# Attention's output, the MLPs and the residual in token-major form: activations as the stationary operand under 512-column weight moves, and per-token norms

## What is computed

```
mod_lat = (silu_c @ ada_w[i] + ada_b[i])[:, None, :]
sh1, sc1, g1, sh2, sc2, g2 = jnp.split(mod_lat, N_MOD, axis=-1)
h_lat = modulate(rms_norm(x, norm_mix_g[i]), sh1, sc1)
if mixer == 0:
    q_l, k_l, v_l = project_qkv(h_lat, ...); k_c, v_c = project_kv(h_ctx, ...)
    o_lat = latent_attention(q_l, k_l, v_l, k_c, v_c) @ attn_w_o[j]
else:
    o_lat = fourier_mix(h_lat, fourier_w_o[j])
x = x + g1 * o_lat
x = x + g2 * sq_relu_mlp(modulate(rms_norm(x, norm_mlp_g[i]), sh2, sc2), mlp_w1[i], mlp_w2[i])
...
return rms_norm(x, final_norm_g)
```

## Time and profile before

| | us |
|---|---|
| median of 3 runs | 2355.04 |
| lowest and highest run | 2353.82, 2355.83 |
| span of the profiled execution | 2354.1 |
| TensorE busy (matmul) | 2174.3 |
| VectorE busy | 1540.7 |
| ScalarE busy | 1057.1 |

### The profile page before, as it was taken

One profiled execution on the slowest core, in us unless ns is written; L12 is line 12 of the kernel. 1 busy time (PEld: TensorE's weight loads), 2 busy tenths in 40 slices (PEclk: granted clock), 3 DMA queues, 4 the chain that ended last, 5 costly groups with the idle time before them and its releaser, 6 DMA issues.

```text
span 2354.1 us, 40722 instructions
## 1 busy us (share of the span) xinstructions
PE 2174.3 (92%) x16563; PEld 2076.8 (88%) x16563; DVE 1540.7 (65%) x1499; ACT 1057.1 (45%) x1302; POOL 170.5 (7%) x245
## 2 busy tenths in 40 slices
PE   5989976679899999999999998989999998999998
PEld 3778864359899999989999988989999998999997
DVE  6868887878776666657777765865444445776554
ACT  4843333433454444444444445345444444444443
POOL 0000000000111111101111100000000000110000
PEclk9989987899999999999999999999999999999998
DMA  9957664248677777767777760965555556774551
GB/s 383 360 208 273 241 224 161 96 145 333 264 268 256 277 248 256 273 231 276 272 258 276 270 246 4 331 249 186 178 179 183 187 182 215 272 275 173 188 180 54
DMA packets 118782, 537.40 MB, mean 228 GB/s; under 512 B 8306, under 2 KB 9124, under 8 KB 97444
## 3 DMA queue, kind: packets, MB, share of 16 engines
q1 hardware_dynamic: 89472, 360.73, 43.0%
q0 software_dynamic: 27136, 167.78, 19.8%
q10 hardware_dynamic: 2084, 7.63, 0.8%
HBM read 534.01 MB, written 2.10 MB: 228 GB/s over the span
## 4 chain that ended last, share of the span: by engine, by line
PE 85%; DVE 9%; ACT 3%; issue 2%; DMA 1%; ACTq 0%; DVEq 0%
PE ps L1021 27%; PE ps L1022 26%; PE ps L1023 26%; DVE w_lo L628 2%; PE ps L1066 2%; DVE hrms L834 2%; DVE ada_sum L647 1%; ACT w_hi L340 1%; DVE nmax L874 1%; PE ps L1107 1%; PE ps L1108 1%; DMA rope<-const_rope 1%; PE ps L1151 1%; PE ps L1144 1%; PE ps L1051 0%
## 5 line engine op out<-in xcount | busy, mean ns | idle before, releaser
L1021 PE MATMUL ps<-h_hi,w_hi 128*128 128x256 f32 x4928 | 1412.2, 287 | 46.0 <-DVE h_lo L741 11.7
L1022 PE MATMUL ps<-h_lo,w_hi 128*128 128x256 f32 x4928 | 1402.8, 285 | 0.0
L1023 PE MATMUL ps<-h_hi,w_lo 128*128 128x256 f32 x4928 | 1402.3, 285 | 0.0
L628 DVE TENSOR_TENSOR w_lo<-raw,w_hi 128x1024 fp32r<-128x1024 f32 x688 | 836.4, 1224 | 666.0 <-ACT w_hi L340 665.9
L340 ACT ACTIVATE w_hi<-raw 128x1024 fp32r<-128x1024 f32 x688 | 723.8, 1058 | 1088.7 <-PE ps L1023 1070.1
L1021 PEld LDWEIGHTS ps<-h_hi,w_hi 128*128 128x128 f32 x4928 | 955.3, 194 | 55.1 <-issue 33.1
L1022 PEld LDWEIGHTS ps<-h_lo,w_hi 128*128 128x128 f32 x4928 | 955.1, 194 | 5.1 <-issue 4.5
L1023 PEld LDWEIGHTS ps<-h_hi,w_lo 128*128 128x128 f32 x4928 | 954.6, 194 | 0.0
L647 DVE SCALAR_TENSOR_TENSOR ada_sum<-ada_raw,silu,ada_sum 128x2048 f32<-128x2048 f32 x120 | 281.6, 2346 | 2.7 <-DMA ada_raw<-in_ada_w 1.9
L294 POOL TENSOR_TENSOR tick<-tick 128x1 f32<-128x1 f32 x80 | 80.4, 1005 | 1196.9 <-DVE ada_sum L647 434.6
L287 POOL DMA_DIRECT2D ada_raw<-in_ada_w x80 | 42.6, 533 | 738.3 <-DVE ada_sum L647 490.2
(11 more groups left out here) (144 smaller groups left out, 1221.9 us busy)
## 6 DMA issues: line engine op xcount, KB each, us to landing
raw<-in_mlp_w SPq DMA_DIRECT2D x256, 1024.0 KB, 4.9
ada_raw<-in_ada_w POOLq DMA_DIRECT2D x160, 1024.0 KB, 5.3
raw<-in_ada_w SPq DMA_DIRECT2D x32, 1024.0 KB, 5.3
raw<-in_attn_w_qkv SPq DMA_DIRECT2D x24, 1024.0 KB, 6.8
raw<-in_attn_w_o SPq DMA_DIRECT2D x16, 1024.0 KB, 5.7
raw<-in_fourier_w_o SPq DMA_DIRECT2D x16, 1024.0 KB, 5.1
x_rows<-in_x ACTq DMA_DIRECT2D x1, 2048.0 KB, 18.5
c_rows<-in_ctx ACTq DMA_DIRECT2D x1, 2048.0 KB, 23.3
```

The lines of the kernel that those rows point to most:

```text
L628: nc.vector.tensor_tensor(w_lo[:, s % SPLIT, :], raw[:, s // 2 % RAW, s % 2, :], w_hi[:, s % SPLIT, :].bitcast(F32), ALU.subtract).then_in ...
L1021: mm(dst, w_h, m_h, start=start, stop=False, skip_group_check=True)
L1022: mm(dst, w_h, m_l, start=False, stop=False, skip_group_check=True)
L1023: return mm(dst, w_l, m_h, start=False, stop=stop, skip_group_check=True)
```

## The change

The program up to the end of attention's head loop stays as it is, but for its buffers and the turning of its modulation vectors. Behind it, and in the ring, this is new:

- The ring `raw` has three buffers in place of four. `h_hi` and `h_lo` become the two halves of one tile `hh` [128, 16, 2, 256], so that high and low part of a channel tile lie side by side. The residual becomes token-major, `x_tm` [128 tokens, 2, 2048 channels].
- **wo and down** (`rows_slice`): the stationary operand is a block of 128 tokens of `h_hi` or `h_lo`, the moving one 512 columns of the weights. A slice takes 12 matmuls of 512 columns. All eight PSUM banks are used, and there is one pass, not two. The last four slices are done bank by bank (`rows_last`), which waits until all four are split.
- **up** (`up_slice`): the weights stay stationary; `w_hi` is met by [high|low] of h in one move of 512 columns, `w_lo` by the high part in one of 256. A slice takes 8 + 8 matmuls. The two halves of the result are added by a copy on ScalarE (`b_half`) and an add on VectorE (`add_halves`). `w1` is now loaded as four rows of 512 numbers per partition, that is in runs of 2 KB, where it was 4 KB.
- **End of a stage** (`stage_end`, on both engines): VectorE multiplies a bank by the gate's row (`g_row`) and adds it to `x_tm`; ScalarE squares it with a running sum, one number per token; root and reciprocal are of one column; `xn` is made by one multiplication per 512 channels and transposed by TensorE (`turn_x`, 4 matmuls for two channel tiles), ScalarE applies scale and shift from PSUM (`modulate`), VectorE splits (`h_split`).
- **Vectors**: a vector that is needed per channel is turned by 16 products of one column (`turn_col`); one that serves as a gate gets its bias on one partition (`add_bias`), is spread over the partitions by four products with ones (`turn_row`) and copied out by ScalarE (`row_out`). Three are turned inside up of layer 0 and one inside up of layer 1. No vector is made in halves. Gate 7 (layer 1) is turned in the Fourier stage.
- At the very end the norm and the gain are applied token-major, with no transposes, and eight DMAs store the result.
- All loops are written out, where up and down had hardware loops, and GpSimd's counting instructions (L294) are gone.

```
-RAW = 4
+RAW = 3
-SUMS = [(0, 2), (0, 3), (0, 4), (1, 0), (1, 1), (1, 2), (0, 5), (1, 3), (1, 4), (1, 5)]
+SUMS = [(0, 2), (0, 3), (0, 4), (1, 0), (1, 1), (0, 5), (1, 3), (1, 2), (1, 4), (1, 5)]
+ROWS = {0: 0, 5: 1, 7: 2, 9: 3}
+COLS = {1: 0, 2: 1, 3: 2, 4: 3, 6: 4, 8: 5}
+UP_STEPS = {0: (4, 5, 6), 1: (9,)}
...
+    x_tm = sb("x_tm", [P, 2, D])
+    hh_at = base[0]
+    hh = sb("hh", [P, KT, 2, T], F32R)
+    xT = place("xT", [P, KT, 2, T], F32, hh_at)[:, :, 1, :]
+    h_hi, h_lo = hh[:, :, 0, :], hh[:, :, 1, :]
+    g_row = sb("g_row", [P, D])
...
+    wo_v = (w_o[0].rearrange("(k p) (h n) -> k p h n", p=P, h=2), fourier_w[0].rearrange("(k p) (h n) -> k p h n", p=P, h=2))
+    w1_v = [w1[l].rearrange("(q k p) (b n) -> b q p k n", p=P, k=4, n=512) for l in range(2)]
+    w2_v = [w2[l].rearrange("(k p) (h n) -> k p h n", p=P, h=2) for l in range(2)]
...
+        def modulate(q, i, bank, shift, gained):
+            act.wait_ge(xT_ready, 8 * q + i + 1)
+            if i == 0:
+                act.wait_ge(a_ready, gained)
+            if 8 * q + i >= 4:
+                act.wait_ge(hl_ready, 8 * q + i - 3)
+            for k in range(2):
+                kt = 2 * i + k
+                act.activation(hT[:, i % 4, k, :], ps[:, bank, k * T:(k + 1) * T], ACT.Identity, bias=shift[:, kt:kt + 1],
+                               scale=a_col[:, q + 2, kt:kt + 1]).then_inc(hT_ready, 1)
...
+            def b_half(blk):
+                bank0 = 4 * (blk % 2)
+                rows = u[:, 4 * blk:4 * blk + 4, :]
+                act.wait_ge(slice_done, 2 * P_UP[l] + 8 * (blk + 1))
+                act.activation(rows, ps[:, bank0:bank0 + 4, T:2 * T], ACT.Copy).then_inc(b_out, 1)
...
+            def relu_square(blk):
+                rows = u[:, 4 * blk:4 * blk + 4, :]
+                act.wait_ge(ab_ready, 16 * l + blk + 1)
+                act.activation(rows, rows, ACT.Relu).then_inc(relu_ready, 1)
+                act.wait_ge(relu_ready, 16 * l + blk + 1)
+                act.activation(rows, rows, ACT.Square).then_inc(u_ready, 1)
...
+        def add_bias(v, row):
+            dve.wait_ge(ada_used, KT * v + KT)
+            dve.wait_ge(bias_in, 16 * (ROWS[v] + 1))
+            nc.vector.tensor_tensor(ada_sum[0:1, :], ada_sum[0:1, :], row[0:1, :], ALU.add).then_inc(biased, 1)
...
+        def take_col(v, bank):
+            lay, m = SUMS[v]
+            col = 96 * lay + 16 * m
+            dve.wait_ge(col_T, COLS[v] + 1)
+            nc.vector.tensor_tensor(mod_col[:, col:col + 16], ps[:, bank, 0:16], bias_col[:, col:col + 16],
+                                    ALU.add).then_inc(mod_ready, 1)
...
+        def gate_bank(q, j):
+            tt, nb = j // 4, j % 4
+            cols = slice(512 * nb, 512 * (nb + 1))
+            if j < 7:
+                dve.wait_ge(bank_full, 7 * q + j + 1)
+            else:
+                dve.wait_ge(slice_done, 2 * P_WO[q // 2] + 32 if q % 2 == 0 else 2 * P_DOWN[q // 2] + 128)
+            if j == 0:
+                dve.wait_ge(row_ready, 4 * q + 4)
+            nc.vector.tensor_tensor(gated[:, j % 2, :], ps[:, 4 * (1 - tt) + nb, :], g_row[:, cols], ALU.mult).then_inc(gated_ready, 1)
+            dve.wait_ge(gated_ready, 8 * q + j + 1)
+            nc.vector.tensor_tensor(x_tm[:, tt, cols], x_tm[:, tt, cols], gated[:, j % 2, :], ALU.add).then_inc(x_blk, 1)
...
+        def h_split(q, i):
+            c0 = 8 * q + i
+            dve.wait_ge(hT_ready, 2 * c0 + 2)
+            nc.vector.tensor_copy(h_hi[:, 2 * i:2 * i + 2, :], hT[:, i % 4]).then_inc(h16_ready, 1)
+            dve.wait_ge(h16_ready, c0 + 1)
+            nc.vector.tensor_tensor(h_lo[:, 2 * i:2 * i + 2, :], hT[:, i % 4], h_hi[:, 2 * i:2 * i + 2, :].bitcast(F32),
+                                    ALU.subtract).then_inc(hl_ready, 1)
...
+        def stage_end(q, next_first, middle=None):
+            for j in range(5):
+                gate_bank(q, j)
+            total(q, 0)
+            gate_bank(q, 5)
+            if next_first:
+                split_lo(next_first)
+            invert(q, 0)
+            gate_bank(q, 6)
+            gate_bank(q, 7)
+            if middle:
+                middle()
+            for b in range(4):
+                if q < 3:
+                    normed(q, 0, b)
+            total(q, 1)
+            invert(q, 1)
+            for b in range(4):
+                if q < 3:
+                    normed(q, 1, b)
...
+            def add_halves(blk):
+                bank0 = 4 * (blk % 2)
+                rows = u[:, 4 * blk:4 * blk + 4, :]
+                dve.wait_ge(b_out, 16 * l + blk + 1)
+                nc.vector.tensor_tensor(rows, ps[:, bank0:bank0 + 4, 0:T], rows, ALU.add).then_inc(ab_ready, 1)
...
+        def turn_col(v, bank):
+            pe.wait_ge(ada_used, KT * (v + 1))
+            for f in range(KT):
+                ins = mm(ps[:, bank, f:f + 1], ada_sum[:, f * P:(f + 1) * P], ones[:, 0:1], start=True, stop=True)
+            ins.then_inc(col_T, 1)
+        def turn_row(v, blocks, bank0):
+            pe.wait_ge(biased, ROWS[v] + 1)
+            for b in blocks:
+                mm(ps[:, bank0 + b, :], ones[:, :], ada_sum[:, 512 * b:512 * (b + 1)], start=True, stop=True).then_inc(row_T, 1)
+        def bank_of(tt, nb):
+            return ps[:, 4 * (1 - tt) + nb, :]
+        def rows_bank(s, k, tt, nb, start, stop, frees=0):
+            tok, cols = slice(tt * P, (tt + 1) * P), slice(512 * (nb % 2), 512 * (nb % 2 + 1))
+            ins = mm(bank_of(tt, nb), h_hi[:, k % KT, tok], w_hi[:, s % SPLIT, cols], start=start, stop=False)
+            if frees:
+                ins.then_inc(slice_done, frees)
+            mm(bank_of(tt, nb), h_hi[:, k % KT, tok], w_lo[:, s % SPLIT, cols], start=False, stop=False)
+            return mm(bank_of(tt, nb), h_lo[:, k % KT, tok], w_hi[:, s % SPLIT, cols], start=False, stop=stop)
+        def rows_slice(first, k, half):
+            s = first + 2 * k + half
+            pe.wait_ge(lo_ready, s + 1)
+            for tt in range(2):
+                for nb in (2 * half, 2 * half + 1):
+                    ins = rows_bank(s, k, tt, nb, k == 0, False)
+            ins.then_inc(slice_done, 1)
+        def rows_last(first, k0):
+            pe.wait_ge(lo_ready, first + 2 * k0 + 4)
+            for tt in range(2):
+                for nb in range(4):
+                    rows_bank(first + 2 * k0 + nb // 2, k0, tt, nb, False, False, 1 if tt == 1 and nb == 2 else 0)
+                    ins = rows_bank(first + 2 * k0 + 2 + nb // 2, k0 + 1, tt, nb, False, True, 2 if tt == 1 and nb == 3 else 0)
+                    if tt == 0 or nb < 3:
+                        ins.then_inc(bank_full, 1)
+            ins.then_inc(slice_done, 1)
...
+        def up_slice(l, blk, p):
+            s = 2 * P_UP[l] + 8 * blk + p
+            pe.wait_ge(lo_ready, s + 1)
+            for a in range(2):
+                k = 2 * p + a
+                for j in range(4):
+                    bank = 4 * (blk % 2) + j
+                    w = slice(512 * a + P * j, 512 * a + P * (j + 1))
+                    mm(ps[:, bank, :].rearrange("p (a t) -> p a t", a=2), w_hi[:, s % SPLIT, w], hh[:, k, :, :], start=(k == 0), stop=False,
+                       skip_group_check=True)
+                    ins = mm(ps[:, bank, 0:T], w_lo[:, s % SPLIT, w], h_hi[:, k, :], start=False, stop=(k == KT - 1),
+                             skip_group_check=True)
+            ins.then_inc(slice_done, 1)
...
+            first = 2 * P_WO[l]
+            if l == 0:
+                pe.wait_ge(o_ready, 16)
+                pe.wait_ge(mod_ready, 2)
+            else:
+                pe.wait_ge(z_ready, 16)
+                pe.wait_ge(y_ready, 8)
+                pe.wait_ge(row_ready, 4 * ROWS[7] + 4)
+            for k in range(KT - 2):
+                for half in range(2):
+                    rows_slice(first, k, half)
+            rows_last(first, KT - 2)
...
+            pe.wait_ge(x_blk, 8 * q + 4)
+            turn_col(v, 7)
+            for i in range(3):
+                turn_pair(i)
+            pe.wait_ge(mod_ready, COLS[v] + 1)
+            turn_pair(3)
+            pe.wait_ge(x_blk, 8 * q + 8)
+            for blk in range(16):
+                if blk == 1:
+                    pe.wait_ge(hT_ready, 2 * (8 * q + 8))
+                if blk >= 2:
+                    pe.wait_ge(ab_ready, 16 * l + blk - 1)
+                for p in range(8):
+                    if blk == 0:
+                        if 1 <= p < 5:
+                            turn_pair(p + 3)
+                        pe.wait_ge(hl_ready, 8 * q + p + 1)
+                    up_slice(l, blk, p)
+                    t = turns(l).get(8 * blk + p)
+                    if t is not None:
+                        pe.wait_ge(ab_ready, 16 * l + blk)
+                        if t in ROWS:
+                            turn_row(t, range(4), 4 * ((blk + 1) % 2))
+                            pe.wait_ge(row_ready, 4 * ROWS[t] + 4)
+                        else:
```

(12 more changed lines are left out.)

789 lines of the change are left out of this document (307 added, 482 removed).

## The result

| | before | changed |
|---|---|---|
| median of the runs, us | 2354.7 (4 runs) | 2295.28 (4 runs) |
| lowest and highest | 2353.82, 2355.83 | 2290.96, 2298.68 |
| span of the profiled execution | 2354.1 | 2296.7 |

The ratio is 0.9741, interval 0.9726 to 0.9757: 59 us, or 2.6%, faster. The forecast of 2294 us is met within 1.3 us. The profiled run itself took 2298.68 us.

A forecast was written before the change was run, and what follows sets the result against it. TensorE, busy for 92% of the span and 85% of the chain, was taken to bound the kernel. The terms sum to -60.9 us against the span of 2354.1, giving 2293.2, and with 0.9 for the median 2294 us; range 2268 to 2326.

The forecast's parts named there:

- last four slices, four times: At four stage ends TensorE waits 2.5 us, uncovered, for slice 31's splits before `rows_last`: +10 us (9 to 14).
- ahead of wo: Three-buffer first stage +4.5, bias and turn between KV and Q +4.5, two `turn_col` beside attention +1.5 each: together +12 us.
- wo to up, twice: From wo to up, VectorE's queue lets up begin after 14.8 us; with half clock and first block 19.3 against 18.8: +1.
- turns inside up: Layer 0: two `turn_col` (4 and 5.5 us) and a `turn_row` (6), +6; layer 1: a new `turn_row`, +4.5; together +10.
- up to down, between sweeps: Shorter wait between up and down -12; pause between sweeps and turn of vector 7 leave down -8: together -20 us.
- Fourier stage and the way to it: Way from down to the Fourier stage 16 us, -5.7; transposes, waits and gate's row in and behind it +7.7: together +2.
- the end: From TensorE's last matmul to the span's end 14.5 us in place of 26.5: -12 us.
- Denser slices: In wo, down and up, 512-column moves take 0.229 us, saving per-matmul extra: -41.6 and -22.3 us (together -82 to -41).
- 2.9 us, too short to lose the clock: Between up and down, copying and adding the last block's half sums takes 2.9 us, without half clock behind it.
- Dearer and cheaper pauses: Stage-end and first-stage pauses: dearer, +28 us, 2322, chance 0.16; cheaper, half clock hidden, -20 us, 2274, chance 0.16.
- Little gain: Widening gives little in wo, down, up: moves 0.240 us, 2358, chance 0.02; weaker form, 2.5 ns per matmul, 2343, chance 0.02.
- Starvation in up: `w1` in 2 KB packets starves up: at 0.175 us per packet +141 and +47 us, 2482; chance 0.06.

The follow-up runs named there:

- experiment 1: The changed kernel with every 512-column move of wo, down and up issued as two of 256 columns, same stationary: 2362.27 us, 1.0026 of the kernel before.
- Experiment 3: The changed kernel with the second and third turns inside up of layer 0 moved to slices 84 and 125, from 82 and 122: 2287.55 us, ratio 0.9703.
- Experiments 4: The changed kernel with the last block of wo and down started at its third split slice, waiting for the fourth only before the third column group: 2287.54 us.
- experiment 6: The changed kernel with VectorE's low split of the next stage's first slice moved behind the gates of banks 6 and 7: 2287.64 us, ratio 0.9706.
- experiment 5: The changed kernel run again without any edit, to see what its time varies by: 2296.19 us, ratio 0.9745.

## Why the prediction was right, and where only its sum was

The working by its own terms, against the changed kernel's first profile:

| term | forecast | measured |
|---|---|---|
| wo and down, 320 slices | -41.6 | -51 |
| up, 256 slices | -22.3 | -21.5 |
| last four slices, four times | +10 | +17 |
| ahead of wo | +12 | +20 |
| wo to up, twice | +1 | -4.5 |
| turns inside up | +10 | +15.5 |
| up to down, between sweeps | -20 | -19 |
| Fourier stage and the way to it | +2 | 0 |
| the end | -12 | -14.5 |
| sum | -60.9 | -58 |

The spans differ by 57.4. The half clock behind a pause counts with the pause, before the change too (1.6 us in up, 2.6 and 3.0 behind the two pauses between up and down).

- **Denser slices.** The mechanism is right, and experiment 1 isolates it. The size for wo and down was short by 10: I took 0.229 per move as a mean over twelve in KV. One by one, in the trace of the kernel before, two of the six kinds of move in that stage are 233 ns apart and the others 226 to 228. The single distances would have shown the bare stream of 226.7 that wo and down then had; the mean did not. For up the forecast is right by accident of the spacing: at 173.3 ns throughout it would have been -27, at 176.7 -14.
- **The last four slices.** The wait was right (2.5; measured 2.46 to 2.56). The half clock behind it, 1.5 to 1.8 us each, was missing. The same error stands in "2.9 us, too short to lose the clock" between up and down: it was lost both times, and only sometimes in later runs. That step failed. I had called those lengths harmless with no row to show it. The kernel before has five pauses of 3.2 to 3.3 us from a turn's start to the next product, three in up and two in down (two are in the earlier trace rows), and TensorE idles for only 1.4 to 2.2 us of each; looked at with the granted clock, one of them was followed by 0.55 and four by 1.00. Two of the five:

```profile
826.00:829.40 3.40, 3.40 (x18) 0.55 0.88 295
730.30:733.70 3.40, 3.33 (x27) 1.00 0.84 289
```

- **Ahead of wo.** The first stage cost 4.4 us to KV's start (forecast 4.5), between KV and Q 5.4 (4.5), the first column 2.6 and the second 2.2 (1.5 each; 32 records of one column take 3.4 us at full clock and 6.6 at half, both inside my bounds of 1.9 and 7.3). Attention itself grew by 4.0 us, which I had at nothing and did not follow up: its cause stays open. The start of wo grew by 1.4 of half clock.
- **Turns.** In order 4.0, 6.2 and 8.2 where I had 4, 6 and 5.5, and half clock behind two of them, 4.4 together. Experiment 3 shows the reason for the second and third.
- **Wo to up.** The 14.8 were right to 0.2 us (14.7 and 15.0), but not for the right reason: I had VectorE's split in the list and not the 1.85 us of waiting for it, and the items around it came out shorter. Experiments 4 and 6 show that it was VectorE's list and not TensorE. What follows up's start (half clock, splits and transposes in its first block) cost 2.4 and 2.0 us, where I had 4.5, and the kernel before lost 2.4 and 2.2 there rather than 1.9.
- **The rivals.** Dearer and cheaper pauses both happened, in different places. *Little gain* is refuted by experiment 1. *Starvation in up* did not come: in up of layer 0 the queue of `raw` took 0.093 us per packet of 2 KB, against 0.175 for mostly 4 KB and the 0.136 at which the whole gain would have been gone:

```profile
q1 hardware_dynamic: 32653, 67.60, 49.5%
q0 software_dynamic: 6912, 50.33, 36.2%
```

(0.495 x 16 x 384 us / 32653, in the stretch from 650 to 1034 us.) Both queues together kept the DMA engines 0.86 busy in that stretch, and TensorE never waited for a piece: in up the least time between landing and use was 2.6 us.

## What to carry to other kernels

Count matmuls, not only columns: in these fp32r streams two of 256 columns cost 13 ns more than one of 512, with the stationary operand new or repeated, and which operand is stationary may be chosen for that. Then read each engine's list at a stage end line by line. Of the 34 us here, all but the 2 to 4 of the fourth buffer lay in orders that no arithmetic asks for: a split between two gates, a wait for four slices where three do, a turn three slices too early, a column sent to the bank that comes free last, a sweep begun with the half whose banks are busy. And price a pause with the half clock behind it, even one of 2.5 us; filling pauses with idle work gained nothing here, removing them did.

## What the runs showed of the hardware that I had not expected

- Pauses of 2.4 to 2.6 us were followed by about 3.4 us at a granted clock of 0.50 in some runs and not in others, at the same place of the same kernel (down of layer 1: 1.6 us apart between the two profiles of the changed kernel). At the two wo ends of experiment 6 it did not fall behind a wait of 2.5 us, at those of the changed kernel it did. The clock also fell in the middle of 32 one-column products that followed each other without a gap (at 637.2, where they run from 634.88 on).
- In up, 512-column and 256-column moves in turn keep one of two spacings for hundreds of microseconds, 173.3 or 176.7 ns per matmul, chosen anew at each stretch. In groups of four they keep a middle value, 175.4, with the long moves 233.6 apart. 256-column moves alone have 120.0 in the kernel before and in experiment 1, and the 512-column moves of wo and down 226.7. What sets the choice stays open.
- Over all stretches of up the choice is worth up to 13 us between two runs, and the clock's behaviour some 6 (the 8.5 us of experiment 5 without the first stage's 1.9 and the 1 that went the other way). Two kernels 5 us apart can't be told apart by four runs each here; their profiles, read place by place, can.
